# Three latent pairs' scores as three one-pass products, with high parts in the weight stages

## The reference

```python
c_q = rms_norm(q_lat, mla_q_norm)
q_m = (c_q @ w_q_b).reshape(B, S, MLA_HEADS, MLA_QK_DIM)            # 8 heads, 96 wide
q_m = jnp.concatenate([q_m[..., :64], apply_rope(q_m[..., 64:], cos_m, sin_m)], axis=-1)
kv = (c_kv @ w_kv_b).reshape(B, S, MLA_HEADS, 128)
k_m = jnp.concatenate([kv[..., :64], jnp.broadcast_to(k_rope, (B, S, MLA_HEADS, 32))], axis=-1)
o_m = blocked_attention(q_m[:, :, :, None, :], k_m, kv[..., 64:], MLA_QK_DIM ** -0.5)
...
s = jnp.einsum('bqkgd,btkd->bkgqt', qblk, k).astype(jnp.float32) * scale   # the scores
p = jax.nn.softmax(s, axis=-1)
```

## Time and profile before

| | |
|---|---|
| median of 3 runs | 2315.43 us (2314.78 to 2318.77) |
| the profiled execution | 2318.02 us, its span 2316.1 |
| busy: TensorE, VectorE, ScalarE, GpSimd | 2279.1, 1323.2, 882.0, 218.4 us |
| granted TensorE clock, mean | 0.996 of full |
| attention of layer 0, units 40 to 63 | 161.2 to 210.0 us |
| values blocks of layer 0 start at | 140.88, 153.64, 167.38, 183.49 |
| those of layer 1 | 728.70 (its second part), 740.04, 753.77, 769.88 |

### The profile page before, as it was taken

One profiled execution on the slowest core, in us unless ns is written; L12 is line 12 of the kernel. 1 busy time (PEld: TensorE's weight loads), 2 busy tenths in 40 slices (PEclk: granted clock), 3 DMA queues, 4 the chain that ended last, 5 costly groups with the idle time before them and its releaser, 6 DMA issues.

```text
span 2316.1 us, 28465 instructions
## 1 busy us (share of the span) xinstructions
PE 2279.1 (98%) x10956; PEld 1640.9 (71%) x10956; DVE 1323.2 (57%) x2063; ACT 882.0 (38%) x1522; POOL 218.4 (9%) x183
## 2 busy tenths in 40 slices
PE   9999999999999999999999999999999999999998
PEld 7756875343775587634467788888888778888887
DVE  5776644233767565423357657777335665877722
ACT  5575542111447554211142334444223234444422
POOL 0212201000221220100000010000001002000000
PEclk9999999999999999999999999999999999999999
DMA  5301539999430143999963233333333423333321
GB/s 185 95 1 46 196 152 380 410 409 410 168 100 5 46 152 145 381 410 410 410 262 105 78 91 95 97 100 94 98 100 136 114 69 91 100 100 99 102 88 58
DMA packets 112662, 381.63 MB, mean 165 GB/s; under 512 B 16528, under 2 KB 17296, under 8 KB 112272
## 3 DMA queue, kind: packets, MB, share of 16 engines
q1 hardware_dynamic: 108928, 367.05, 45.2%
q0 software_dynamic: 2304, 8.39, 0.9%
q10 hardware_dynamic: 1296, 4.37, 0.5%
HBM read 363.51 MB, written 6.29 MB: 160 GB/s over the span
## 4 chain that ended last, share of the span: by engine, by line
PE 87%; DVE 5%; ACT 3%; DMA 2%; POOL 1%; issue 1%; SPq 0%; POOLq 0%; DVEq 0%; ACTq 0%
PE ps L1384 11%; PE ps L1386 11%; PE ps L1385 11%; PE ps L1691 9%; PE ps L1408 5%; PE ps L1410 5%; PE ps L1409 5%; PE ps L1713 4%; PE ps L1572 3%; PE ps L1427 3%; PE ps L1429 3%; PE ps L1428 3%; PE ps L1522 2%; PE ps L1530 2%; DMA wa<-in_wu 1%; PE ps L1723 1%
## 5 line engine op out<-in xcount | busy, mean ns | idle before, releaser
L2524 DVE TENSOR_TENSOR wlo<-stage,whi 128x1024 fp32r<-128x1024 f32 x262 | 328.0, 1256 | 268.8 <-ACT whi L1836 268.0
L1384 PE MATMUL ps<-hTh,whi 128*128 128x512 f32 x1120 | 441.0, 394 | 0.1
L1386 PE MATMUL ps<-hTh,wlo 128*128 128x512 f32 x1120 | 436.3, 390 | 0.0
L1385 PE MATMUL ps<-hTl,whi 128*128 128x512 f32 x1120 | 436.0, 389 | 0.0
L1836 ACT ACTIVATE whi<-stage 128x1024 fp32r<-128x1024 f32 x262 | 275.9, 1057 | 325.1 <-PE ps L1410 120.7
L1384 PEld LDWEIGHTS ps<-hTh,whi 128*128 128x128 f32 x1120 | 210.3, 188 | 48.1 <-issue 4.9
L1386 PEld LDWEIGHTS ps<-hTh,wlo 128*128 128x128 f32 x1120 | 210.2, 188 | 44.6
L1385 PEld LDWEIGHTS ps<-hTl,whi 128*128 128x128 f32 x1120 | 210.3, 188 | 42.3
L2436 DVE TENSOR_TENSOR ps<-ps,Rs 128x512 f32<-128x512 f32 x124 | 86.0, 698 | 140.1 <-PE ps L1386 126.2
L2439 DVE SCALAR_TENSOR_TENSOR t<-ps,vecs,t 128x511 f32<-128x511 f32 (+1 forms) x176 | 131.1, 745 | 3.8 <-ACT t L1793 0.7
L2436 DVE TENSOR_TENSOR x<-x,ps 128x512 f32<-128x512 f32 x184 | 116.4, 680 | 28.4 <-PE ps L1410 18.0
(11 more groups left out here) (387 smaller groups left out, 4218.9 us busy)
## 6 DMA issues: line engine op xcount, KB each, us to landing
stage<-in_wpk SPq DMA_DIRECT2D x268, 512.0 KB, 3.6
wa<-in_wd SPq DMA_DIRECT2D x56, 512.0 KB, 15.5
wa<-in_wu SPq DMA_DIRECT2D x54, 512.0 KB, 15.0
wa<-in_wg SPq DMA_DIRECT2D x46, 512.0 KB, 14.3
ws<-in_wg SPq DMA_DIRECT2D x26, 512.0 KB, 12.5
ws<-in_wu SPq DMA_DIRECT2D x24, 512.0 KB, 11.8
wr<-in_wg SPq DMA_DIRECT2D x24, 512.0 KB, 15.1
stage<-in_wd SPq DMA_DIRECT2D x22, 512.0 KB, 16.3
```

The costliest lines, as they stand in the source:

```text
L1384: pe.matmul(o, h, ah, start=k == 0, stop=False)
L1385: pe.matmul(o, h, al, start=False, stop=False)
L1386: t = pe.matmul(o, lo, ah, start=False, stop=k == 7)
L2524: ve.tensor_tensor(M.wlo[i % NW][:, :], M.stage[i % NSTAGE][:, :], f(M.whi[i % NW][:, :]), ALU.subtract).then_inc(*S.wlo.mark(("w", i)))
```

## The change

The scores of the last three latent pairs (p = 5, 6, 7; units 40 to 63) become three one-pass products: high·high, high·low, low·high. Pair 4 stays float32. A table LAT_HI places twelve new high parts (lat_hi, ScalarE, a 128x512 copy) into units 31 to 53, and their low parts (lat_lo, VectorE, a 128x512 difference, written over mq and mk in place) one unit later. The high parts lie in the stage tiles of four weight chunks: 38l+15 and +16 for pair 6, 38l+17 and +18 for pairs 5 and 7. So `hold` stops the loads at chunk 38l+15 from the start of the mixer; at unit 57 two loads are issued that wait for the scores of unit 55, at unit 63 the rest up to six ahead of the split, which wait for the scores of unit 63.

```diff
--- before.py
+++ after.py
@@ -16,6 +16,8 @@
 NSTAGE = 6
 NW = 3
 LAG = 5
+LAT_HI = {31: (5, 0, 1), 33: (5, 0, 0), 35: (5, 1, 1), 37: (5, 1, 0), 39: (6, 0, 1), 40: (6, 0, 0), 44: (6, 1, 1), 45: (6, 1, 0),
+          48: (7, 0, 1), 49: (7, 0, 0), 52: (7, 1, 1), 53: (7, 1, 0)}
 NS = 39
 N1 = 13
 
@@ -109,6 +111,7 @@
         self.turn = 0
         self.cur = self.loaded = self.split = 0
         self.limit = NCH
+        self.hold = NCH
         self.rel = set()
         self.held = None
         self.sbank = {}
@@ -144,7 +147,7 @@
 
     def load(self, after=None):
         i = self.loaded
-        if i >= min(NCH, self.limit):
+        if i >= min(NCH, self.limit, self.hold):
             return
         self.loaded += 1
         self.do("load", i, after)
@@ -408,6 +411,7 @@
     def mixer(self, l):
         s = ("mix", l)
         self.do("point", "mixer", l)
+        self.hold = 38 * l + 15
         self.rb = [(0, None), (1, None)]
         ns = 3 * l
         ready = self.head(ns, s)
@@ -512,6 +516,14 @@
                     self.do("key_dup", l, g)
             elif 0 < j < 4 and r < 4:
                 self.do(("head_hi", "head_lo")[r % 2], l, "q%d" % j, r // 2)
+            if n in LAT_HI:
+                self.do("lat_hi", l, *LAT_HI[n])
+            if n - 1 in LAT_HI:
+                self.do("lat_lo", l, *LAT_HI[n - 1])
+            if n in (57, 63):
+                self.hold = 38 * l + 17 if n == 57 else NCH
+                for _ in range(2 if n == 57 else self.split + NSTAGE - self.loaded):
+                    self.load(("scores", "mix", l, 55 if n == 57 else 63))
             if n in halves:
                 self.do("whi_half", l, self.split, halves[n])
             if n - 1 in halves:
@@ -1116,6 +1128,8 @@
         self.y1l = A("y1l", 0, [128, 4, 512], F32R)
         self.mq = at("mq", OH, [128, 8, 512])
         self.mk = at("mk", OH + 16 * KB, [128, 8, 512])
+        self.ml = [at("mql", OH, [128, 8, 512], F32R), at("mkl", OH + 16 * KB, [128, 8, 512], F32R)]
+        self.mh = [at(f"mh{i}", OST + 2 * KB * i, [128, 512], F32R) for i in range(2 * NSTAGE)]
         Pr = [A(f"Pr{i}", (32, 42)[i] * KB, [128, 512]) for i in range(2)] + self.tmp[2:4]
         PT = [A(f"PT{i}", (60, 68, 34, 52)[i] * KB, [128, 4, 512]) for i in range(4)]
 
@@ -1209,7 +1223,14 @@
             q, j = self.qs[2 * p + h], p // 2
             return [(q, self.kh[j][:, :]), (q, self.kl[j][:, :])], lambda kt: self.vg[:, kt, 64 * j:64 * j + 64]
         j = 2 * (p - 4) + h
+        if p > 4:
+            (qh, kh), (ql, kl) = (self.high(l, p, h, w) for w in range(2)), (t[:, j, :] for t in self.ml)
+            return [(qh, kh), (qh, kl), (ql, kh)], lambda kt: self.vm[:, kt, 64 * j:64 * j + 64]
         return [(self.mq[:, j, :], self.mk[:, j, :])], lambda kt: self.vm[:, kt, 64 * j:64 * j + 64]
+
+    def high(self, l, p, h, w):
+        c = 38 * l + (15 if p == 6 else 17) + h
+        return self.mh[2 * (c % NSTAGE) + w][:, :]
 
     def expert(self, l, i):
 
@@ -1511,6 +1532,10 @@
                 q.wait_ge(*S.dup[p // 2].at("dup", l))
                 q.wait_ge(*S.act.at("heads", l, f"q{p}", h))
                 q.wait_ge(*S.dve.at("heads", l, f"q{p}", h))
+            elif p > 4:
+                for w in (1, 0):
+                    q.wait_ge(*S.act.at("lat_hi", l, p, h, w))
+                    q.wait_ge(*S.dve.at("lat_lo", l, p, h, w))
             else:
                 g = 2 * (p - 4) + h
                 q.wait_ge(*S.act.at("mq", l, g))
@@ -1913,6 +1938,23 @@
             l, p, u, i = a
             q.wait_ge(*S.pe.at("mk", l, p))
             copy(M.mk[0:64, 2 * p, :], M.ps[u[0]][0:64, :], ("mk", l, p), ("free",) + u)
+        elif name == "lat_hi":
+            l, p, h, w = a
+            g = 2 * (p - 4) + h
+            if w:
+                q.wait_ge(*S.act.at("mk", l, p - 4))
+                q.wait_ge(*S.dve.at("mk", l, p - 4))
+                q.wait_ge(*S.mk[p - 4].at("mk", l))
+            else:
+                q.wait_ge(*S.act.at("mq", l, g))
+                q.wait_ge(*S.dve.at("mq", l, g))
+            if p == 7:
+                q.wait_ge(*S.pe.at("scores", "mix", l, 47))
+            else:
+                c = 38 * l + (15 if p == 6 else 17) + h - NSTAGE
+                q.wait_ge(*S.whi.at("w", c))
+                q.wait_ge(*S.wlo.at("w", c))
+            copy(M.high(l, p, h, w), (M.mk if w else M.mq)[:, g, :], ("lat_hi", l, p, h, w))
         elif name == "vm":
             l, m, u, i = a
             q.wait_ge(*S.pe.at("vm", l, m))
@@ -2317,7 +2359,9 @@
             if i >= NSTAGE:
                 q.wait_ge(*S.whi.at("w", i - NSTAGE))
                 q.wait_ge(*S.wlo.at("w", i - NSTAGE))
-            if after:
+            if after and after[0] == "scores":
+                q.wait_ge(*S.pe.at(*after))
+            elif after:
                 q.wait_ge(*S.pe.at("e", *after[1:]))
             sp.dma_start(M.stage[i % NSTAGE][:, :], M.dram["wpk"][i]).then_inc(*S.stage[i % NSTAGE].mark(("load", i)))
         elif name == "start2":
@@ -2651,6 +2695,17 @@
             q.wait_ge(*S.pe.at("mq", l, h))
             stt(M.mq[64:128, h, :], M.ps[u[0]][64:128, :], 96 ** -0.5, M.mcs[64:128, :], ALU.mult, ALU.mult, ("mq", l, h),
                 ("free",) + u)
+        elif name == "lat_lo":
+            l, p, h, w = a
+            g = 2 * (p - 4) + h
+            q.wait_ge(*S.act.at("lat_hi", l, p, h, w))
+            if w:
+                q.wait_ge(*S.dve.at("mk", l, p - 4))
+                q.wait_ge(*S.mk[p - 4].at("mk", l))
+            else:
+                q.wait_ge(*S.dve.at("mq", l, g))
+            tt(M.ml[w][:, g, :], (M.mk if w else M.mq)[:, g, :], f(M.high(l, p, h, w)), ALU.subtract,
+               ("lat_lo", l, p, h, w))
         elif name == "mk":
             l, p, u, i = a
             q.wait_ge(*S.pe.at("mk", l, p))
```

## The result

| | before | after |
|---|---|---|
| median | 2317.1 us (2314.78 to 2318.91, 4 runs) | 2332.13 us (2331.02 to 2333.53, 4 runs) |
| span of the profiled execution | 2316.1 | 2331.7 |

The ratio is 1.0063, interval 1.0051 to 1.0075. The forecast was no change; 2332.1 lies 11 us above the end of the range.

What follows compares the result with a forecast made beforehand. TensorE was taken as the bound, VectorE second at 73%. Saving 8.0 us against 8.0 lost (4.0 a layer each) left 2315.4 us, no change; range 2308.0 to 2321.0.

Steps and rivals of the forecast that it cites:

- the loads: Four weight chunks a layer load later: cost 0, up to 3.6 us a chunk if uncovered; late-chunk rival, chance 0.02.
- the queries' pairs: Existing high-low pairs in the grouped units, two ahead of each values block: cost 1.0 us, 0.5 each.
- What a difference waits for its high part: Units 37 to 44: each VectorE difference waits about 0.3 us for ScalarE's high part; stretch loss taken as 0.8 us.
- The free 2.5 us: Attention loop: VectorE can fall some 2.5 us behind in eight units, and the values block lets it catch up.
- Units 45 to 52: GpSimd's norm chain and VectorE's scaling queued behind two differences: 1.5 us lost a layer, bounds 0.5 and 1.9.
- Units 53 to 64: Two differences, a half chunk and late gain products lose 0.4 us; the gap for GpSimd's square loses 0.3.
- The port: Rival: differences meeting GpSimd on the shared port add 1.5 us of VectorE a layer; 3.0 slower, 2318.4; chance 0.10.
- VectorE's queue: Rival: each difference costs TensorE its whole 0.61 us, mainly units 45 to 60; 7.8 slower, 2323.2; chance 0.11.
- ScalarE's copies: Twelve high-part copies a layer: 7.4 us of ScalarE time counted, no loss priced for them.
- The products: Latent units at 1.13 us instead of 1.30: 4.0 us saved a layer, 8.0 in both.
- room-enough rival: VectorE's delays stay in the free room, only two GpSimd links cost 0.3 each a layer; 2308.6; chance 0.22.
- The clock: TensorE's clock stood at 1.00 throughout the stretch of units 40 to 63, so nothing comes from there.

Runs made afterwards that it cites:

- e1: Changed kernel with only its late loads kept, no splits and no three products: 2317.55 us against 2317.10 for the kernel before.
- e8: Changed kernel with GpSimd's four subtractions (y low) in each layer's output norm replaced by memsets: 2327.36 us against 2317.28 before.
- e4: Changed kernel with every low part three units behind its high part instead of one: 2324.67 us against 2317.10 before.
- e11: Changed kernel with low parts three units behind high parts and GpSimd's four subtractions a layer replaced by memsets: 2320.39 us against 2317.11 before.
- e7: Changed kernel with high parts alone, no low parts; products read the unsplit value instead: 2315.54 us against 2317.28 before.
- e2: Changed kernel without splits: late loads and three one-pass products of unsplit values: 2311.64 us against 2317.10 before.
- e3: Changed kernel with all splits and late loads, but one float32 product of the low parts per tile: 2331.51 us against 2317.10 before.
- e5: Changed kernel with high-low pairs moved behind the values of units 20, 28, 36, 44 and 52: 2332.60 us against 2317.28 before.
- e9: Changed kernel with two high-low pairs ahead of the values of units 12, 20, 28, 36, 44 and 52: 2321.31 us against 2317.11 before.

## Why the prediction was wrong

**Right.** The pitch of 1.13 us; the loads at nothing (e1); that the losses would show as waits of the values for VectorE's copy behind units 36 and 44, and at GpSimd's link to the column sums; that layer 1 repeats layer 0 (7.0 and 7.2). VectorE stayed under the 85% that I had named for a bound engine: 40.68 us of the 49.0 between 161 and 210, 83%.

**The step that failed: the losses by stretch, which I sized by the queries' pairs and by VectorE's mean room.** I took 4.0 us a layer; 11.1 were lost, against 4.1 saved. The table has the losses of each stretch in layer 0, the shift of the aligned traces plus 0.17 us for each latent unit (sums taken before rounding); layer 1 agrees within 0.2 us.

| units | 29 to 36 | 37 to 44 | 45 to 52 | 53 to 60 | 61 to 63 | sum |
|---|---|---|---|---|---|---|
| predicted | 1.0 | 0.8 | 1.5 | 0.4 | 0.3 | 4.0 |
| after | 2.4 | 2.2 | 4.3 | 1.8 | 0.3 | 11.1 |
| e8, memset | 2.4 | 2.2 | 3.4 | 0.8 | 0.3 | 9.2 |
| e4, gap of three | 0.6 | 1.4 | 1.9 | 3.1 | 0.3 | 7.4 |
| e11, both | 0.6 | 1.4 | 1.9 | 1.1 | 0.3 | 5.4 |
| e7, high parts only | 0.5 | 0.0 | 1.4 | 0.6 | 0.3 | 2.9 |
| e2, products only | 0.0 | 0.0 | 0.9 | 0.2 | 0.3 | 1.4 |

**What a difference waits for its high part.** I took 0.3 us, and for units 29 to 36 the 1.0 us of the queries' pairs (bounds 0 and 1.5). Measured: 0.77 and 0.20 us ahead of the copy that unit 36's values need, with two differences, 2.2 us in all, and 2.4 for the stretch. Units 37 to 44 were 0.8; measured a shift of +1.4, with 0.85 saved on five units, so 2.2. Both lie outside their bounds. The rows on which I priced it have a low part ahead of the needed copy too, but only one, and it waits 0.21 us; the other waits 0.90, but while the values run. Timeline of before, at the values behind unit 28, whose second head begins at 142.30:

```profile
140.74 0.69 DVE L2439 SCALAR_TENSOR_TENSOR qs<-raw,qs 64x512 fp32r<-64x512 f32 x1 [0.21 <-ACT qs L1793]
...
144.25 0.69 DVE L2439 SCALAR_TENSOR_TENSOR qs<-raw,qs 64x512 fp32r<-64x512 f32 x1 [0.90 <-ACT qs L1793]
```

I took the neighbour's pitch as that of the same kind without looking at where its high parts stood in ScalarE's queue and its low parts in VectorE's.

**The free 2.5 us.** I counted VectorE's room over eight units. But the copy PT that the values need is a deadline within one unit of the differences, and what VectorE catches up later doesn't undo TensorE's wait.

**Units 45 to 52.** 1.5 taken (bounds 0.5 and 1.9) out of the saving; measured a shift of +2.9 (3.8 to 6.7) with 1.4 saved: 4.3. The links were the right ones, but GpSimd's squares waited for an oT behind a difference, its sum took 1.60 us beside another (1.27 in the earlier trace rows), the values behind unit 52 waited for a copy behind the 1.81 us row, and the clock fell. This is the largest miss of all, 2.8 us.

**Units 53 to 64.** 0.4 + 0.3 taken, measured +0.3 with 1.9 saved: 2.2, with two long records of VectorE in it (1.72 us at 196.92 and 1.15 at 199.75).

**The port.** A rival with 0.10, worth 1.5 us a layer of VectorE's time. It measured 2.7 us a layer of VectorE's time, and 1.3 to 2.4 of the path (e8). I read two meetings, found one long and one short, and averaged them at 0.6. The trace agreed in both, not in one: the short one too ends 0.55 us behind GpSimd's row, of which little was left (it ended at 193.43; GpSimd's sum, begun at 191.61, at 192.88). The rule that fits all rows here is the one above, and y's subtractions follow the gain products so closely that a difference beside them pays nearly the whole 1.1 us. "VectorE's queue" was the rival nearest to the truth (2323.2), but it too left out the waits and the port.

**ScalarE's copies.** 0 taken, 3.7 us measured (e7; 2.9 by the aligned traces), in units 29 to 36, 45 to 52 and 53 to 60.

**The products** were to save 4.0 a layer. Alone they save 2.7 of 4.1. The links of the room-enough rival (0.6) took 0.8, and the values behind units 52 and 60 the other 0.5.

**The clock.** "Nothing comes from there" was wrong in after: 3.4 us at half speed from 184.1 us, behind the 1.05 us in which TensorE stood, and again from 774.6. Were TensorE the bound there, that would be up to 3.4 / 2 = 1.7 us a layer. It is not what makes the loss: e3 has no such segment in the attentions and loses the same 7.1 us in layer 0, and e8 keeps both and gets 4.9 us back. But e4 has neither, so part of its 7.5 us, up to 3.4, may have come by way of the clock; no run separates that.

By steps, each run against the next: e2 -5.5; ScalarE's copies +3.7 (e7, -1.7); VectorE's plain time +5.0 (e11, +3.3); the port and the places of the differences, waits for high parts included, +11.7 (the changed kernel, +15.0), of which the port 4.9 (part of it the kernel's own) and the differences' places 7.5, alone (the waits for high parts some 3.8 of it). The intervals reach 2 to 2.5 us to either side of a difference for the runs taken eight times or more and 3 to 4 for the changed kernel, e3, e4, e5 and e8, so the two small terms are rough. By the table the 5.0 lie in units 37 to 44 (1.4 us a layer), 45 to 52 (0.5) and 53 to 60 (0.6).

## What to carry to other kernels

Price an added pair of instructions on two in-order queues (one makes, the other uses) by where the first stands in its own queue and by what is ready behind the second: 0.93 us of waiting ahead of a copy that a full TensorE needs within a few units cost 0.9 (units 37 to 44, after against e4), and 1.36 us inside a block of values cost nothing (the same units in e9), where nothing else was due. Look for the nearest deadline of that queue, not for its mean room: VectorE at 73% beside a TensorE at 99% had none where the differences stood. And count every overlap with GpSimd's reads of SBUF as what is left of GpSimd's instruction.

## What the hardware showed beyond that

- A VectorE tensor-tensor with both inputs in SBUF ended 0.55 us behind the end of GpSimd's tensor-tensor that had begun before it (1.81 and 1.15 us instead of 0.69), and was not slowed by a memset of GpSimd that had (0.68). GpSimd pays as well: its sum took 1.60 us behind such a difference that had begun first, and 1.27 without.
- GpSimd's 128x512 difference of two SBUF tensors takes 1.28 us, 1.9 times VectorE's 0.69.
- A stall of TensorE of about 1 us (1.05) ahead of a column sum was followed by 3.4 us at the lower clock level (1.2 GHz, granted 0.50); in e4, where TensorE stood 1.30 us ahead of the transposes at 182.03, it stayed up. The length of one stall alone doesn't decide. Windows of e4:

```profile
182.00:192.00 10.00, 9.96 (x54) 6.78 (x55) 8.68 (x13) 7.31 (x17) 4.84 (x3) 1.00 0.00 0
177.00:184.00 7.00, 5.57 (x40) 4.41 (x38) 5.68 (x12) 5.54 (x14) 2.31 (x3) 1.00 0.00 0
```
